# A decode step's page loads, old x, output weights and last stores put in another order

## The chip, the cores and the metric

The kernel runs on one core of a Trainium2 chip, in one launch. The metric is device time in microseconds; the number given for a kernel is the median of its runs. A separate execution is recorded by the hardware profiler, and the rows further down come from it.

## What is computed

Two layers of a decoder trunk, for 512 prompt tokens and for 8 sequences of 8 new tokens each. Every sequence of new tokens attends to 16 cached pages of 128 rows, which a page table places in a pool. Cut to what matters here:

```python
def layer_forward(x, pos, p, ret_s0, ret_chunk, attend):
    h = rmsnorm(x, p['norm_w'])
    z = h @ p['w_in']                       # 1024 -> 3264 columns
    ...                                     # retention on half the heads
    o_a = attend(qn, qp, c, kpe, p)         # latent attention
    y = jnp.concatenate([o_r, o_a], axis=-1) @ p['w_out']
    return x + y, c, kpe, s_new

def mla_attend_sample(...):                 # one of 8 sequences
    c_all  = concat([cache_ckv[layer, pt].reshape(-1, 256), c_s])
    kp_all = concat([cache_kpe[layer, pt].reshape(-1, 64), kpe_s])
    kn = rmsnorm(c_all @ w_kb); v = c_all @ w_vb
    s = qn @ kn.T + qp @ kp_all.T           # then mask, softmax
    return softmax(s * SCALE) @ v
```

## The kernel before

Everything is fp32, and the large products are made of three TensorE products of a high and a low part. Each layer goes through four stages: the input projection in eight column groups; the prompt's attention and the retention; the eight decode sequences over their cached pages; and the output projection in three column groups (344, 340 and 340 columns) over five row tiles. Tiles 0 to 3 are the prompt's, 128 rows each; tile 4, `S_TILE`, holds the 64 new tokens.

**The program of each engine is written out by hand**, and the engines meet at semaphores. All DMAs are issued by SyncE (SP), in program order; a wait holds back everything written behind it.

**The decode stage.** Page buffers are double: `ckv[b]` and `kp[b]` hold the 16 pages of one sequence, sequence s in buffer s mod 2. `load_seq(seq, b, wait)` asks for them in four quarters of four pages. A quarter is four reads of the page table, then, unless `wait` is None, one wait on `pv_ps` (the quarter of the sequence two before has been multiplied by its probabilities, so its pages are free), then eight DMAs: four of 32 KB (`kp`) and four of 128 KB (`ckv`).

TensorE works through a sequence in eight page pairs `q`. In pair `q` it transposes the pages of pair q+1 (`turn_pair`, line 978) and multiplies the keys of pair q (`pair_keys`, line 1003). The softmax of the sequence before is worked off meanwhile: in pair 4 `tail_attend` (line 1031) multiplies its probabilities by its pages and frees its buffer; in pair 6 `tail_turn` (line 1051) transposes the result; in pair 7 the first pages of the next sequence are transposed, and this waits for their DMAs.

**SP's order in the decode stage** is: pages of sequence 0; `wout0` (first column group of the output weights); pages of sequence 1; old x (`z[:, :, 0:D]`, 2 MB of prompt and 256 KB of new tokens, needed for the residual sum at the end of the layer); `wout1` (second column group, four DMAs of 340 KB); in the first layer a wait and the clearing of the layer's semaphores, followed by `fresh`; then a loop over the pages of sequences 2 to 7.

**The output projection.** `out_product(g, t)` makes column group g of tile t. A prompt tile takes 24 matmuls, `S_TILE` 16. VectorE adds a tile to old x (`x_add`, line 2128). For `S_TILE` its high and low rows are summed first: ScalarE copies the low half out of PSUM (`move_out`, line 1560) and VectorE adds twice (lines 2126 and 2128). `store(g)` waits for `S_TILE` of group g and writes the group's columns with two DMAs, one for four prompt tiles and one for `S_TILE`.

Of the kernel before, what the change touches and what calls it, by code (L numbers as in the profile page):

```python
# [30 lines left out]
DEPTH, D, SEQ = 2, 1024, 512  # L31
NB, NT = 8, 8
# [3 lines left out]
TILES = SEQ // P + 1  # L36
S_TILE = TILES - 1
# [14 lines left out]
OG = (0, 344, 684, 1024)  # L52
# [12 lines left out]
def rows(t):  # L65
    return ST if t == S_TILE else P
# [50 lines left out]
def build(nc, x_prompt, x_sample, cache_ckv, cache_kpe, state_ret, page_table, norm_w, w_in, q_a_norm_w,  # L117
# [177 lines left out]
    def sem(name, per_layer=True):  # L295
        s = nc.alloc_semaphore(name)
        if per_layer:
            layer_sems.append(s)
        return s
# [10 lines left out]
        + [(2, t) for t in range(TILES)]  # L310
    NTH = {gt: i + 1 for i, gt in enumerate(OUT_ORDER)}
    N_OUT = len(OUT_ORDER)
    N_W = 4 * (NG + 3)
    N_RAW = NG + 1
    N_Y = 2 * TILES
# [4 lines left out]
    def mix_tile(k):  # L320
# [10 lines left out]
    out_done, state_out, x_out = sem("out_done"), sem("state_out"), sem("x_out", False)  # L331
# [39 lines left out]
    y_ready, y_turned, y_hi, y_lo, out_ps, x_new = (sem(n) for n in  # L371
        ("y_ready", "y_turned", "y_hi_kept", "y_lo_kept", "out_in_psum", "x_new_ready"))
# [8 lines left out]
    X_OUTS = 6  # L381
# [5 lines left out]
    def zc(t, c0, n):  # L387
        return z[0:rows(t), t, c0:c0 + n]
# [3 lines left out]
    def _(sp):  # L392
        yp_t = y_prompt[0].rearrange("(t p) d -> p t d", p=P)
        ys_t = y_sample.rearrange("b t d -> (b t) d")
# [7 lines left out]
        def load_norm(l):  # L402
            spread(norm_b[:, :], norm_w, l, D, norm_in)
# [36 lines left out]
        for L in range(DEPTH):  # L440
            for g in range(1, NG):
                for k in range(4):

                    sp.wait_ge(w_lo_ok, N_W * L + g * 4 + (k - 3))
                    sp.dma_start(raw[:, k, :, :], w_in_t[L][:, 2 * k:2 * k + 2, g * GW:(g + 1) * GW])\
# [31 lines left out]
            def load_seq(seq, b, wait, quarters=range(QUARTERS)):  # L477
                for k in quarters:
                    numbers = [load_page(seq, b, k * QPAGES + n) for n in range(QPAGES)]
                    if wait is not None:  # L480

                        sp.wait_ge(pv_ps, (wait + L * NB) * QUARTERS + (k + 1))
                    for n, v in enumerate(numbers):
                        sp.dma_start(kp[b][:, k * QPAGES + n, :], kpe_rows[bass.ds(v, 1), :, :]  # L484
                                     .rearrange("l p k -> (l p) k")).then_inc(page_in[QUARTERS * b + k], 16)
                        sp.dma_start(ckv[b][:, k * QPAGES + n, :], ckv_rows[bass.ds(v, 1), :, :]  # L486
                                     .rearrange("l p k -> (l p) k")).then_inc(page_in[QUARTERS * b + k], 16)
# [15 lines left out]
            load_seq(1, 1, None)  # L503


            if L:
                sp.wait_ge(x_out, 16 * X_OUTS)
            old_p = yp_t if L else x_prompt[0].rearrange("(t p) d -> p t d", p=P)
            old_s = ys_t if L else x_sample.rearrange("b t d -> (b t) d")
            sp.dma_start(z[:, 0:S_TILE, 0:D], old_p).then_inc(xold_in, 16)  # L510
            sp.dma_start(z[0:ST, S_TILE, 0:D], old_s).then_inc(xold_in, 16)

            for k in range(4):
                sp.dma_start(wout1[:, k, :, :], w_out_t[L][:, 2 * k:2 * k + 2, OG[1]:OG[2]]).then_inc(wout1_in, 16)
            if L + 1 < DEPTH:
# [3 lines left out]
                    if s not in running_sems:  # L519
                        sp.sem_clear(s)  # L520
                sp.sem_inc(fresh, 1)
            with sp.Fori(1, NB // 2) as i:
                load_seq(i * 2, 0, i * 2 - 2)
                load_seq(i * 2 + 1, 1, i * 2 - 1)

# [6 lines left out]
            def store(g):  # L532
                cols = slice(OG[g], OG[g + 1])
                sp.wait_ge(x_new, N_OUT * L + NTH[g, S_TILE])
                sp.dma_start(yp_t[:, :, cols], z[:, 0:S_TILE, cols]).then_inc(x_out, 16)
                sp.dma_start(ys_t[:, cols], z[0:ST, S_TILE, cols]).then_inc(x_out, 16)

            if L + 1 < DEPTH:

                sp.wait_ge(out_ps, N_OUT * L + NTH[0, S_TILE])  # L540
                load_norm(L + 1)
                load_small(L + 1)
                store(0)
                for k in range(4):

                    sp.wait_ge(w_lo_ok, N_W * L + 4 * (NG + 2) + k + 1)
                    sp.dma_start(raw[:, k, :, :], w_in_t[L + 1][:, 2 * k:2 * k + 2, 0:GW]).then_inc(raw_in[k], 16)
            else:
                store(0)
            store(1)  # L550
            store(2)
        sp.wait_ge(x_out, 16 * X_OUTS * DEPTH)


    @block.tensor
    def _(pe):
# [7 lines left out]
        def tile_products(out, t, w_h, w_l, chunks=range(DC), w0=None):  # L564

            for c in chunks:
                if w0 is not None and c % 2 == 0:
                    pe.wait_ge(w_lo_ok, w0 + c // 2 + 1)
                if t == S_TILE:
                    pe.matmul(out, hT_s[:, c, :], w_h(c), start=c == 0, stop=False)  # L570
                    m = pe.matmul(out, hT_s[:, c, :], w_l(c), start=False, stop=c == DC - 1)  # L571
                else:
                    rows_t = slice(t * P, (t + 1) * P)
                    m = product(out, (hT_hi[:, c, rows_t], hT_lo[:, c, rows_t]), (w_h(c), w_l(c)), c == 0, c == DC - 1)
            return m
# [3 lines left out]
        for L in range(DEPTH):  # L579
# [15 lines left out]
            def tile_product(g, t):  # L595
# [7 lines left out]
                for chunks in halves:  # L603
                    if chunks[0]:
                        x_turn(1)
                    m = tile_products(ps[:, BANK[t], 0:GW], t, lambda c: w_hi[w][:, c, :], lambda c: w_lo[w][:, c, :],
                                      chunks, w0=N_W * L if g == 0 and t == 0 else None)
                m.then_inc(z_in_psum, 1)
# [7 lines left out]
            for g in range(1, NG):  # L616
                pe.wait_ge(w_lo_ok, N_W * L + g * 4 + 4)
                for t in range(TILES):
# [478 lines left out]
            def out_chunks(g, t, chunks):  # L1097
                n_cols = OG[g + 1] - OG[g]
                if g == 0:
                    w_h, w_l = w0_hi, w0_lo  # L1100
                else:
                    w_h, w_l = w_hi[W_PAR[g]], w_lo[W_PAR[g]]
                return tile_products(ps[:, BANK[t], 0:n_cols], t, lambda c: w_h[:, c, 0:n_cols],
                                     lambda c: w_l[:, c, 0:n_cols], chunks)

            def out_begin(g, t):
                if g == 0:
                    if t == 0:
                        pe.wait_ge(w_lo_ok, N_W * L + 4 * (NG + 1))
                    pe.wait_ge(y_lo, N_Y * L + 2 * (t + 1))  # L1110

                    if t < 2:
                        pe.wait_ge(kk_kept, 2 * N_PAIR * (L + 1) - 1)
                    elif t < S_TILE:
                        pe.wait_ge(kk_kept, 2 * N_PAIR * (L + 1))
                    else:
                        pe.wait_ge(rp_kept, N_PAIR * (L + 1))
                else:
                    if t == 0:
                        pe.wait_ge(w_lo_ok, N_W * L + 4 * (NG + g + 1))  # L1120
                    pe.wait_ge(x_new, N_OUT * L + NTH[g - 1, t])
                out_chunks(g, t, range(DC // 2))

            def out_end(g, t):
                out_chunks(g, t, range(DC // 2, DC)).then_inc(out_ps, 1)

            def out_product(g, t):
                out_begin(g, t)
                out_end(g, t)
# [36 lines left out]
            out_product(0, S_TILE)  # L1166
            for t in range(1, TILES):
                out_product(1, t)
            for t in range(S_TILE):
                out_product(2, t)  # L1170
            if L + 1 < DEPTH:
                pe.wait_ge(fresh, L + 1)
                x_turn(0)
            out_product(2, S_TILE)


    @block.scalar
    def _(act):
# [11 lines left out]
        for L in range(DEPTH):  # L1190

            def square_x(t):
                if L == 0:
                    act.wait_ge(x_in[t], 16)
                else:
                    act.wait_ge(x_new, N_OUT * (L - 1) + NTH[2, t])
                act.activation(zc(t, D, D), zc(t, 0, D), ACT.Square, accum_out=stat[0:rows(t), t:t + 1])
# [7 lines left out]
            def split(g, chunks=range(4)):  # L1205
                for k in chunks:
# [3 lines left out]
                    if k == 0 and g < 2 and L:  # L1210

                        act.wait_ge(out_ps, N_OUT * (L - 1) + NTH[1 + g, S_TILE])
                    act.wait_ge(raw_in[k], 16 * (N_RAW * L + g + 1))
# [339 lines left out]
                    act.activation(dst[:, 2 * k:2 * k + 2, 0:n], src, ACT.Copy).then_inc(w_hi_ok, 1)  # L1553

            def move_out(g, L):
                act.wait_ge(out_ps, N_OUT * L + NTH[g, S_TILE])
                if g:
                    act.wait_ge(x_new, N_OUT * L + NTH[g - 1, S_TILE])
                n_cols = OG[g + 1] - OG[g]
                act.activation(out_s[:, 0:n_cols], ps[ST:P, BANK[S_TILE], 0:n_cols], ACT.Copy).then_inc(out_s_moved, 1)  # L1560
# [43 lines left out]
    def _(dve):  # L1604
# [18 lines left out]
        for L in range(DEPTH):  # L1623
# [495 lines left out]
            def x_add(g, t, L):  # L2119
                n = rows(t)  # L2120
                n_cols = OG[g + 1] - OG[g]
                dve.wait_ge(out_ps, N_OUT * L + NTH[g, t])
                x = zc(t, OG[g], n_cols)
                if t == S_TILE:
                    dve.wait_ge(out_s_moved, 3 * L + g + 1)
                    dve.tensor_tensor(x, out_s[:, 0:n_cols], x, ALU.add)
                    dve.drain()
                dve.tensor_tensor(x, ps[0:n, BANK[t], 0:n_cols], x, ALU.add).then_inc(x_new, 1)
# [69 lines left out]
            x_add(1, S_TILE, L)  # L2198
            x_add(2, 0, L)
            if L + 1 == DEPTH:  # L2200
                for t in range(1, TILES):
                    x_add(2, t, L)


# [215 lines left out]
```

## Time and profile before

| what | us |
|---|---|
| median of 3 runs (1241.48 to 1242.68) | 1241.63 |
| profiled execution, its own time | 1244.96 |
| its span, first to last instruction | 1243.2 |
| TensorE (PE) busy in it | 1215.2 |
| VectorE, ScalarE, GpSimd busy | 724.2, 527.2, 436.3 |

The profiled execution has 1.76 us around its span, and its own time is 3.33 us above the median of the runs. PE is busy for 98% of the span, with a mean granted clock of 0.996 of full speed, so the kernel goes as fast as PE is fed; what can be won lies in the 28 us in which PE does not work and in the stretches in which its clock is lower.

### The profile page before, as it was taken

The page shows a single profiled execution, that of the slowest core. Times are in us where ns is not written, and L with a number is a line of the kernel's source. Part 1 is how long each engine was busy: PE and PEld are TensorE (multiplying, and loading weights), DVE is VectorE, ACT ScalarE, POOL GpSimd, SP SyncE. Part 2 cuts the span into 40 slices and gives each one's busy share as a digit, 9 for nine tenths or more (in the row PEclk, how much of TensorE's full clock was granted, in tenths as well). Part 3 has the DMA queues.
Part 4 walks back from the last instruction along what each step waited for, and adds up shares of the span by engine and source line. Part 5 has one row for each costly group of instructions (what it writes and reads, how often), then busy time and mean ns, then how long its engine had stood idle before and what let it go on. Part 6 is the DMA issues. An engine that isn't in the chain of part 4 may idle for free.

```text
span 1243.2 us, 26204 instructions
## 1 busy us (share of the span) xinstructions
PE 1215.2 (98%) x8720; PEld 1127.1 (91%) x8720; DVE 724.2 (58%) x1322; ACT 527.2 (42%) x1377; POOL 436.3 (35%) x632
## 2 busy tenths in 40 slices
PE   6999999999989999999999999999999999999998
PEld 6999995768989999999999999867789999999998
DVE  5455746565646666666463465656556566665652
ACT  4311325444645555563242122453455555555520
POOL 1023046432535454541010320554235445454400
PEclk9999999999989999999999999999999999999999
DMA  9331104103462223220733130220045433322021
GB/s 318 115 108 55 54 2 123 37 1 95 131 186 77 78 79 85 75 54 1 260 119 123 55 109 1 76 85 1 13 134 157 130 85 84 84 75 75 21 72 51
DMA packets 127894, 108.32 MB, mean 87 GB/s; under 512 B 45681, under 2 KB 123634, under 8 KB 127794
## 3 DMA queue, kind: packets, MB, share of 16 engines
q1 hardware_dynamic: 127794, 107.08, 28.9%
q8 instruction: 51, 0.84, 0.3%
q14 instruction: 49, 0.40, 0.1%
HBM read 96.12 MB, written 10.91 MB: 86 GB/s over the span
## 4 chain that ended last, share of the span: by engine, by line
PE 81%; SPq 9%; issue 3%; DVE 2%; DMA 2%; ACT 1%; DVEq 1%; POOL 0%; POOLq 0%; ACTq 0%
PE ps L1003 23%; PE ps L560 10%; PE ps L561 10%; PE ps L562 10%; PE ps L978 4%; PE ps L654 3%; SPq L486 3%; SPq L470 3%; PE ps L570 3%; PE ps L571 3%; SPq L484 2%; PE ps L1031 2%; PE ps L1012 1%; PE ps L813 1%; PE ps L667 1%
## 5 line engine op out<-in xcount | busy, mean ns | idle before, releaser
L2049 DVE TENSOR_REDUCE kss<-ksq 128x8 f32<-128x1024 f32 x128 | 156.0, 1219 | 171.1 <-ACT ksq L1525 171.0
L560 PE MATMUL ps<-w_hi,hT_hi 128*128 128x408 f32 (+2 forms) x704 | 242.9, 345 | 1.5 <-DVE hT_lo L1614 1.5
L1525 ACT ACTIVATE ksq<-ps 128x544 f32<-128x544 f32 x256 | 160.1, 625 | 196.3 <-PE ps L1003 195.9
L561 PE MATMUL ps<-w_lo,hT_hi 128*128 128x408 f32 (+2 forms) x704 | 240.0, 341 | 0.0
L562 PE MATMUL ps<-w_hi,hT_lo 128*128 128x408 f32 (+2 forms) x704 | 239.3, 340 | 0.0
L1003 PE MATMUL ps<-wq_hi,cT_hi 128*128 128x272 f32 x1024 | 224.7, 301 | 0.0
L2384 POOL TENSOR_TENSOR krs<-kss_t,cst 128x8 f32<-128x8 f32 x128 | 210.0, 1640 | 20.1 <-issue 4.2
L1003 PE MATMUL ps<-wq_lo,cT_hi 128*128 128x272 f32 x1024 | 212.6, 289 | 0.0
L1003 PE MATMUL ps<-wq_hi,cT_lo 128*128 128x272 f32 x1024 | 212.6, 289 | 0.0
L1003 PEld LDWEIGHTS ps<-wq_lo,cT_hi 128*128 128x128 f32 x1024 | 161.7, 190 | 0.0
L1003 PEld LDWEIGHTS ps<-wq_hi,cT_lo 128*128 128x128 f32 x1024 | 161.4, 189 | 0.0
L1003 PEld LDWEIGHTS ps<-wq_hi,cT_hi 128*128 128x128 f32 x1024 | 160.0, 190 | 0.0
L560 PEld LDWEIGHTS ps<-w_hi,hT_hi 128*128 128x128 f32 x704 | 132.6, 188 | 2.8 <-DVE hT_lo L1614 1.9
L561 PEld LDWEIGHTS ps<-w_lo,hT_hi 128*128 128x128 f32 x704 | 132.9, 189 | 0.1
L562 PEld LDWEIGHTS ps<-w_hi,hT_lo 128*128 128x128 f32 x704 | 132.7, 189 | 0.2
L2377 POOL TENSOR_TENSOR kss_t<-kss,cst 128x8 f32<-128x8 f32 x128 | 27.2, 212 | 246.6 <-DVE kss L2049 246.6
L1220 ACT ACTIVATE z<-ps 64x408 f32<-64x408 f32 x16 | 8.1, 508 | 226.0 <-PE ps L571 226.0
L1512 ACT ACTIVATE cT_hi<-ps 128x512 fp32r<-128x512 f32 x126 | 76.6, 608 | 39.5 <-PE ps L978 39.4
L2041 DVE TENSOR_TENSOR cT_lo<-ps,cT_hi 128x512 fp32r<-128x512 f32 x126 | 86.0, 683 | 5.8 <-ACT cT_hi L1512 5.3
L2209 POOL TENSOR_SCALAR pool_tmp<-stat 128x1 f32<-128x1 f32 (+2 forms) x70 | 17.1, 244 | 194.3 <-ACTq L1198 77.6
L978 PE MATMUL ps<-cst,ckv 128*128 128x128 f32 x504 | 79.0, 280 | 6.2 <-DMA ckv<-in_cache_ckv 4.9
L1652 DVE TENSOR_SCALAR z<-ps 128x408 f32<-128x408 f32 x64 | 35.9, 579 | 81.6 <-PE ps L562 80.2
(209 smaller groups left out, 1989.9 us busy)
## 6 DMA issues: line engine op xcount, KB each, us to landing
ckv<-in_cache_ckv SPq DMA_DIRECT2D x256, 128.0 KB, 2.0
raw<-in_w_in SPq DMA_DIRECT2D x64, 408.0 KB, 4.4
kp<-in_cache_kpe SPq DMA_DIRECT2D x256, 32.0 KB, 1.8
S<-in_state_ret SPq DMA_DIRECT2D x8, 512.0 KB, 6.2
out<-S SPq DMA_DIRECT2D x8, 512.0 KB, 3.2
wout<-in_w_out SPq DMA_DIRECT2D x8, 344.0 KB, 4.5
z<-in_w_out SPq DMA_DIRECT2D x8, 340.0 KB, 10.1
raw<-in_w_out SPq DMA_DIRECT2D x8, 340.0 KB, 4.3
```

The costliest lines, as they stand in the source:

```text
L470: v = sp.value_load(pages[0:1, seq * NPAGE + n:seq * NPAGE + n + 1] if isinstance(seq, int) else pages[0:1, bass.ds(seq * NPAGE + n, 1)], ...
L486: sp.dma_start(ckv[b][:, k * QPAGES + n, :], ckv_rows[bass.ds(v, 1), :, :] .rearrange("l p k -> (l p) k")).then_inc(page_in[QUARTERS * b + ...
L560: pe.matmul(out, a_hi, b_hi, start=first, stop=False)
L561: pe.matmul(out, a_hi, b_lo, start=False, stop=False)
L562: return pe.matmul(out, a_lo, b_hi, start=False, stop=last)
L978: m = pe.transpose(ps[:, 0, (2 * j + c) * P:(2 * j + c + 1) * P], ckv[b][:, 2 * q + j, c * P:(c + 1) * P], ident)
L1003: m = pe.matmul(ps[:, 1 + 2 * j + side, 0:CUT], x, w[:, c, w0:w0 + CUT], start=c == 0 and k == 0, stop=c == KC - 1 and k == 2)
L1512: act.activation(cT_hi[:, par, :, :].rearrange("p a n -> p (a n)"), ps[:, 0, :], ACT.Copy)\
L1525: act.activation(ksq[:, q % 2, j, :].rearrange("p (s c) -> p s c", s=2), ps[:, 1 + 2 * j:3 + 2 * j, 0:CUT], ACT.Square).then_inc(kk_sq, 1)
L2041: dve.tensor_tensor(cT_lo[:, par, :, :].rearrange("p a n -> p (a n)"), ps[:, 0, :], cT_hi[:, par, :, :].rearrange("p a n -> p (a n)").bitc ...
L2049: dve.tensor_reduce(kss[:, hs, 2 * k:2 * k + 2, :], ksq[:, q % 2, :, c0:c0 + HW].rearrange("p j (h k) -> p j h k", h=H), AX.X, ALU.add).th ...
L2384: pool.tensor_tensor(krs[:, hs, c, :], tmp, spread_col(neg_half[:, 0:1]), ALU.pow)\
```

## The change

There are two parts. In SP's program, the pages of sequence 2 are asked for ahead of old x, and those of sequence 3 ahead of `wout1`; the loop starts at the pair of sequences 4 and 5. In the last layer's last column group, the order of the tiles is 0, 1, 2, `S_TILE`, 3 in place of 0, 1, 2, 3, `S_TILE`, on TensorE, on VectorE and in the counts that ScalarE waits for; and each tile is stored by a DMA of its own as soon as it is added.

```diff
+    LAST_TILES = (0, 1, 2, S_TILE, 3)
+
+    def nth(g, t, L):
+        if g == 2 and L + 1 == DEPTH:
+            return N_OUT - TILES + 1 + LAST_TILES.index(t)
+        return NTH[g, t]
...
             load_seq(1, 1, None)
+            load_seq(2, 0, 0)
             if L:
                 sp.wait_ge(x_out, 16 * X_OUTS)
...
             sp.dma_start(z[:, 0:S_TILE, 0:D], old_p).then_inc(xold_in, 16)
             sp.dma_start(z[0:ST, S_TILE, 0:D], old_s).then_inc(xold_in, 16)
+            load_seq(3, 1, 1)
...
-            with sp.Fori(1, NB // 2) as i:
+            with sp.Fori(2, NB // 2) as i:
                 load_seq(i * 2, 0, i * 2 - 2)
                 load_seq(i * 2 + 1, 1, i * 2 - 1)
...
-            store(2)
-        sp.wait_ge(x_out, 16 * X_OUTS * DEPTH)
+            if L + 1 < DEPTH:
+                store(2)
+        for t in LAST_TILES:
+            sp.wait_ge(x_new, N_OUT * (DEPTH - 1) + nth(2, t, DEPTH - 1))
+            dst = ys_t[:, OG[2]:OG[3]] if t == S_TILE else yp_t[:, t, OG[2]:OG[3]]
+            sp.dma_start(dst, zc(t, OG[2], OG[3] - OG[2])).then_inc(x_out, 16)
+        sp.wait_ge(x_out, 16 * (X_OUTS * DEPTH - 2 + TILES))
...
-            for t in range(S_TILE):
-                out_product(2, t)
             if L + 1 < DEPTH:
+                for t in range(S_TILE):
+                    out_product(2, t)
                 pe.wait_ge(fresh, L + 1)
                 x_turn(0)
-            out_product(2, S_TILE)
+                out_product(2, S_TILE)
+            else:
+                for t in LAST_TILES:
+                    out_product(2, t)
...
-                act.wait_ge(out_ps, N_OUT * L + NTH[g, S_TILE])
+                act.wait_ge(out_ps, N_OUT * L + nth(g, S_TILE, L))
...
-                dve.wait_ge(out_ps, N_OUT * L + NTH[g, t])
+                dve.wait_ge(out_ps, N_OUT * L + nth(g, t, L))
...
-                for t in range(1, TILES):
+                for t in LAST_TILES[1:]:
                     x_add(2, t, L)
```

SP's program of the first layer, where the last page DMA of sequence 1 (`kp1`, `ckv1`) stands, before the change. The `ISA` rows of line 520 are the wait and the clearing of semaphores.

```order
L486 DMA ckv1_118<-in_cache_ckv 128x256
L510 DMA z_49<-in_x_prompt 128x4x1024
L511 DMA z_49<-in_x_sample 64x1024
L514 DMA z_49<-in_w_out 128x2x340 x4
L520 ISA [waits half_scores_ready]
L520 ISA x74
L522 UNCONDITIONAL_BRANCH
L522 ISA
L470 TENSOR_LOAD pages_64
```

The same place after the change, with the first page-table read and the first wait and DMAs of sequence 2; old x stands behind its 32 DMAs:

```order
L493 DMA ckv1_118<-in_cache_ckv 128x256
L477 TENSOR_LOAD pages_64
...
L491 ISA [waits latents_attended_a_quarter]
L491 DMA kp0_119<-in_cache_kpe 128x64
...
L493 DMA ckv0_117<-in_cache_ckv 128x256
L518 DMA z_49<-in_x_prompt 128x4x1024
L519 DMA z_49<-in_x_sample 64x1024
L477 TENSOR_LOAD pages_64
```

And where the loop is entered after the change, behind the last page of sequence 3; the page buffer asked for next (`kp0`) is that of sequence 4:

```order
L493 DMA ckv1_118<-in_cache_ckv 128x256
L523 DMA z_49<-in_w_out 128x2x340 x4
L529 ISA [waits half_scores_ready]
L529 ISA x74
L531 UNCONDITIONAL_BRANCH
L531 ISA
L477 TENSOR_LOAD pages_64
...
L491 ISA [waits latents_attended_a_quarter]
L491 DMA kp0_119<-in_cache_kpe 128x64
```

Old x moved behind the 32 DMAs of sequence 2, and the output weights with the 75 semaphore instructions moved from the entry of sequence 2's pages to that of sequence 4's. Each layer's program has 64 page DMAs more outside the loop; the number that is executed is the same.

The end of VectorE's program before, from the first column group 2 tile of 64 rows onward:

```order
L2128 TENSOR_TENSOR z_49<-ps,z_49 128x340 [waits out_in_psum] x4
L2126 TENSOR_TENSOR z_49<-z_49 64x340 [waits out_sample_lo_moved,out_in_psum]
L2128 TENSOR_TENSOR z_49<-ps,z_49 64x340
L2395 UNCONDITIONAL_BRANCH
```

and after the change:

```order
L2145 TENSOR_TENSOR z_49<-ps,z_49 128x340 [waits out_in_psum] x3
L2143 TENSOR_TENSOR z_49<-z_49 64x340 [waits out_sample_lo_moved,out_in_psum]
L2145 TENSOR_TENSOR z_49<-ps,z_49 64x340
L2145 TENSOR_TENSOR z_49<-ps,z_49 128x340 [waits out_in_psum]
L2412 UNCONDITIONAL_BRANCH
```

The two adds of `S_TILE` (64 rows) moved ahead of the last add of a prompt tile. The last stores on SP became, after the change:

```order
L565 DMA out_0<-z_49 128x340 [waits x_new_ready] x3
L565 DMA out_1<-z_49 64x340 [waits x_new_ready]
L565 DMA out_0<-z_49 128x340 [waits x_new_ready]
L2412 UNCONDITIONAL_BRANCH [waits x_out]
```

Four stores of 170 KB and one of 85 KB stand there in place of one of 680 KB and one of 85 KB.

## Rows read from the trace of the kernel before

**Rows 1.** The page: busy time of each engine.

```profile
PE 1215.2 (98%) x8720; PEld 1127.1 (91%) x8720; DVE 724.2 (58%) x1322; ACT 527.2 (42%) x1377; POOL 436.3 (35%) x632
```

**Rows 2.** Waits, whole run: engine, line, awaited, total us, times, longest.

```profile
PE ps L978 <- DMA ckv<-in_cache_ckv: 4.9, 2, 3.3
```

**Rows 3.** PE timeline, first layer: start, us, instruction [idle before <-releaser].

```profile
359.87 1.11 PE L978 MATMUL ps<-cst,ckv 128*128 128x128 f32 x4 [3.27 <-DMA ckv<-in_cache_ckv]
```

**Rows 4.** Windows around that stall: us, busy by engine, PEclk, DMA share, GB/s.

```profile
356.60:359.87 3.27, 0.01 (x1) 0.01 (x1) 1.22 (x1) 0.27 (x3) 1.59 (x3) 0.87 0.47 130
359.87:366.36 6.49, 6.49 (x32) 6.49 (x32) 0.89 (x3) 1.48 (x4) 0.44 (x1) 0.54 0.40 102
366.36:370.09 3.73, 3.73 (x34) 3.73 (x33) 1.82 (x2) 2.20 (x7) 1.46 (x3) 1.00 0.25 69
```

**Rows 5.** Windows from one line-1031 group to the next; layer one, then two.

```profile
346.27:385.52 39.25, 35.98 (x302) 35.02 (x305) 20.88 (x33) 18.64 (x58) 16.60 (x25) 0.91 0.47 136
385.52:418.50 32.98, 32.98 (x301) 32.13 (x305) 20.78 (x33) 18.57 (x58) 16.53 (x25) 1.00 0.30 81
...
959.85:994.74 34.89, 33.30 (x302) 32.35 (x305) 20.88 (x33) 18.65 (x58) 16.60 (x25) 1.00 0.52 153
```

**Rows 6.** SP timeline, first layer, behind the last page of sequence 1.

```profile
340.12 1.93 SPq L510 DMA_DIRECT2D z<-in_x_prompt  x1
...
342.67 2.29 SPq L514 DMA_DIRECT2D z<-in_w_out  x4
352.52 0.35 SPq L484 DMA_DIRECT2D kp<-in_cache_kpe  x1
```

**Rows 7.** The chain that ended last, just behind: start, us, what.

```profile
357.31 2.43 DMA ckv<-in_cache_ckv
```

**Rows 8.** SP timeline in the loop: first and last DMAs of sequences 3, 4.

```profile
386.30 0.34 SPq L484 DMA_DIRECT2D kp<-in_cache_kpe  x1
...
389.91 0.33 SPq L486 DMA_DIRECT2D ckv<-in_cache_ckv  x1
...
410.65 0.33 SPq L486 DMA_DIRECT2D ckv<-in_cache_ckv  x1
...
419.30 0.35 SPq L484 DMA_DIRECT2D kp<-in_cache_kpe  x1
```

**Rows 9.** PE timeline, where sequence 3's first pages are used.

```profile
395.59 0.64 PE L978 MATMUL ps<-cst,ckv 128*128 128x128 f32 x4
```

**Rows 10.** Tile ckv: all its DMAs, issue time on SP, then landing.

```profile
L486 SPq DMA_DIRECT2D ckv<-in_cache_ckv x256: 332/333/2052, 285.0 to 1152.7; - x128
DMA to landing us min/median/max: 1.9/2.0/6.9
```

**Rows 11.** The chain and PE timeline, second layer, third sequence's first pages.

```profile
965.55 6.10 DMA ckv<-in_cache_ckv
971.76 0.65 PE L978 MATMUL ps<-cst,ckv 128*128 128x128 f32 x4 [1.59 <-DMA ckv<-in_cache_ckv]
```

**Rows 12.** Window of the large loads, second layer; columns as in rows 4.

```profile
955.00:970.00 15.00, 15.00 (x150) 14.15 (x148) 8.68 (x15) 7.99 (x25) 7.73 (x10) 1.00 1.00 309
```

**Rows 13.** Timeline of the end: PE, ACT, DVE, SP.

```profile
1236.98 0.31 PE L571 MATMUL ps<-w_lo,hT_s 128*128 128x340 f32 x1
1237.33 0.45 ACT L1560 ACTIVATE z<-ps 64x340 f32<-64x340 f32 x1 [17.07 <-PE ps L571]
...
1238.46 0.50 DVE L2128 TENSOR_TENSOR z<-ps,z 64x340 f32<-64x340 f32 x1
1238.99 0.39 SPq L535 DMA_DIRECT2D out<-z  x1
1239.43 0.51 SPq L536 DMA_DIRECT2D out<-z  x1
```

**Rows 14.** SP's own waits at the end, same columns as rows 2.

```profile
SPq L2395 <- DMA out<-z: 2.8, 1, 2.8
```

**Rows 15.** The chain: a 256 KB store with the queue to itself.

```profile
923.04 2.60 DMA out<-S
```

## The prediction

> **What bounds the kernel now.** I read the page first: PE works for 1215.2 of 1243.2 us [rows 1], so only what makes PE wait, or lowers its clock, or follows its last matmul, can move the time. The table of waits then says which of PE's waits the change can touch: line 978, the transposes of fresh pages, waited for page DMAs twice, 4.9 us in all, 3.3 the longest [rows 2]. The timeline places them: once in each layer, both times at the first pages of the third sequence (sequence 2). PE stood still for 3.27 us before 359.87 in the first layer [rows 3] and for 1.59 us before 971.76 in the second [rows 11].
>
> Windows over that place show a second loss. In the first layer the granted clock was 0.87 of full during the stall, 0.54 in the 6.49 us after it, and 1.00 again from 366.36 [rows 4]: PE had fallen from 2.4 to about 1.2 GHz. A page pair that takes 3.73 us at the full clock took 6.49 there, 2.76 us more. In the second layer, after 1.59 us of standstill, the clock stayed at 1.00: the window that holds the second layer's stall reads 1.00 throughout [rows 5].
>
> The cleanest measure is the period of the decode stage, from one group of line 1031 to the next. It is 32.98 us where nothing disturbs it, and the next one, whose end is 451.54, is 33.04, so I take 33.01. Around the third sequence it is 39.25 us in the first layer and 34.89 in the second [rows 5]. **The excess is 6.24 us and 1.88 us, 8.12 together**; in the first, 3.27 is standstill, 2.76 slow clock and 0.2 the restart.
>
> Why were the pages late? In the first layer SP issued old x from 340.12, `wout1` from 342.67, then worked through the semaphore clearing and the page table until its first page DMA at 352.52 [rows 6]. The last `ckv` DMA of the quarter went out at 357.31 and landed 2.43 us later [rows 7]. The buffer had been free since about 347: `tail_attend` began at 346.27 [rows 5], and in the loop the first DMA follows it by 0.78 us (386.30 after 385.52) [rows 5, 8]. So SP's order held the pages back, not the buffer. In the second layer, without the clearing, the last `ckv` DMA was issued at 965.55, but took 6.10 us to land [rows 11], against a median of 2.0 [rows 10]: it stood behind 3.6 MB of old x and `wout1`, while the DMA engines were busy for the whole stretch (share 1.00, 309 GB/s) [rows 12].
>
> **The pages of sequence 2.** They will be asked for right behind those of sequence 1, that is at 340.12 in place of old x; SP reads four page numbers and then waits until the first quarter is free, at 346.27 + 0.78 = 347.05. From then on a quarter takes what it takes in the loop: first DMA to last `ckv` DMA 3.61 us (386.30 to 389.91) [rows 8], landing 2.0 [rows 10]. Landed: 352.7. PE needs them when its standstill began, 359.87 - 3.27 = 356.60 [rows 3], so 3.9 us are to spare. The loop's own margin agrees: needed at 395.59 [rows 9], landed at 389.91 + 2.0 = 391.9, 3.7 us to spare. The second layer's stall began at 970.17 [rows 11] and its pages would land at 959.85 + 0.78 + 3.61 + 2.0 = 966.2: 4.0 to spare. Both stalls go, and with the first the slow clock. I take the full excess, 8.12 us; not less, because nothing but the pages separates those two periods from the others, and not more, because PE works for all of 32.98 us in an undisturbed period [rows 5].
>
> **Old x and `wout1`, later.** Old x now goes out behind the last DMA of sequence 2. A sequence's 32 DMAs take 24.35 us (386.30 to 410.65) [rows 8], so at about 347.05 + 24.35 = 371.4; with its 2.5 us of issue [rows 6] and four page numbers SP is ready for sequence 3 at about 377. That sequence's release is at 386.30 - 6.24 = 380.06. No delay. The data are first used by the sum at the end of the layer, behind all eight sequences. Its 2.25 MB at the 309 GB/s of [rows 12] take 7.3 us and are through by about 381, as the first pages go out. Cost: nothing; the cover is those 3 us and the margin of 3.7.
>
> **The semaphore clearing, later.** This is the step with least room. From the first `wout1` DMA to the first page DMA behind the clearing SP took 352.52 - 342.67 = 9.85 us [rows 6]. After the change that stands between the last DMA of sequence 3, at 410.65 - 6.24 = 404.4 plus 0.4, and the first of sequence 4: 414.65. The buffer is free for it at 419.30 - 6.24 = 413.06 [rows 8]. So those pages start 1.6 us late. The first quarter at a loop entry also took longer, 4.79 us to its last `ckv` issue (352.52 to 357.31) against 3.61: 1.2 more. Late by 2.8 in all, of the 3.7 there are: it is hidden, with 0.9 us left. Later quarters are needed one every two page pairs, twice 3.73 us [rows 4], and go out faster than that. ScalarE, GpSimd and PE wait for `fresh` only at the end of the layer. Second layer: no clearing, no delay.
>
> **The end.** PE's last matmul begins at 1236.98 and ends at 1237.29, whichever tile it belongs to, since the same 112 matmuls are issued. Before, ScalarE's copy at 1237.33 and VectorE's two adds followed, the second from 1238.46 to 1238.96; the stores were issued at 1238.99 and 1239.43 [rows 13], SP waited 2.8 us for them [rows 14], from 1239.94 to 1242.74, and the span ended at 1243.2, 5.91 us after PE. After, tile 3 needs one add: 1237.33 to 1237.84, store issued at 1237.87. `S_TILE` is through by then: its copy and adds take 1.7 us and tile 3's 24 matmuls 3.8.
>
> No row shows a store of 170 KB with the queue to itself. The nearest is one of 256 KB, 2.60 us [rows 15]; from below I take the 2.0 of a 128 KB page [rows 10], from above the 85 KB store at the end, 1242.74 - 1239.43 = 3.31, though it went behind 680 KB. With 2.60 the data are down at 1240.47 and the span ends 0.46 later, at 1240.93: **a gain of 2.27 us**, between 1.56 and 2.87. The three earlier stores in pieces are 3.8 us apart or 2.5 (one tile's matmuls) and end before it.
>
> The Trainium skill speaks against splitting a store: "DMA: Bandwidth & Descriptors", the rules for kernel authors, wants small transfers coalesced, and its anatomy of one DMA gives a fixed part of about 2.0 us to each. By its formula a 174 KB store takes 2.4 us, an estimate from that page, and the end would gain 2.5; the four fixed parts would be paid at the same time as PE's matmuls. The trace's 680 KB store does not show the two parts apart.
>
> **The sum.** 6.24 + 1.88 + 2.27 = 10.39 us off the profiled execution: span 1232.8, own time 1234.6. The runs of before have a median 3.33 us below that execution; taking the same difference off, **1241.63 - 10.4 = 1231.2**. Its own range, from the end's bounds and a few tenths at each stall, is 1230.2 to 1232.4.
>
> **Rivals.**
> *The slow clock is not in the timed runs (0.20).* The profiled execution was 3.33 us slower than the runs, and 2.76 of that may be this very stretch. For it: the size, and that the second layer's standstill of 1.59 us did not lower the clock [rows 5, 11], so a standstill need not. Against: recording an execution costs something by itself, and this stall is twice as long as the harmless one. Then the gain is 7.6 and the time 1234.0. "TensorE: Matmul & The Clock Gate", what's actually happening, in the Trainium skill, says that the moment at which the clock is judged runs freely, so the same kernel can differ from run to run. One execution with one fall and one without agrees and proves nothing.
>
> *A new stall at sequence 4 in the first layer (0.12).* The 0.9 us left are an estimate, and one `ckv` issue sometimes took up to 2.05 us in place of 0.33 [rows 10]. One more such hiccup (1.7) makes PE wait 0.8: 1232.0; with the clock falling too, 2.76 more, 1234.8.
>
> *The order was not what held the pages (0.04).* Then both stalls stay and only the end gains: 1239.4, within 0.2% of before.
>
> *Slower (0.03).* The large loads now go out in the middle of the stream of pages. If pages land behind them as in the second layer before, 6.10 us, they outlast the 2.0 + 3.7 us that there are. There are four such places (old x and `wout1`, two layers). The point that decides is a landing of more than 5.7 us together with a fallen clock: each stall as heavy as the first layer's costs 6.24, and two give back 12.5, 1243.7. Against it: the pages are asked for 6 us or more after the load's issue, not 3.
>
> **How the numbers follow.** The forecast has 0.58, and 0.03 is left for what I haven't seen. The range takes in the clock rival and most of the stall: 1229.8 to 1235.6. A measurement of this kernel tells about 0.2%, 2.5 us, from no change; forecast, clock and stall all lie beyond it: faster 0.91, same 0.06, slower 0.03.
>
> **What the changed kernel's profile would show.** Line 978 waits for no `ckv` DMA, or under 1 us; PEclk is 1.00 in every window from 300 to 1230; periods of 33.0 us at both third sequences; the first page DMAs of sequence 2 about 0.8 us behind line 1031's group; those of sequence 4 in the first layer about 1.6 us late; from PE's last matmul to the end 3.6 us. A wait at line 978 near 416 would show the clearing was not hidden; a timed gain near 7.6 with the profile as forecast would point to the clock; a last store of over 3.3 us would make the end's term wrong.

## The result, and the profile after

The changed kernel took 1234.45 us (median of 4 runs, 1234.08 to 1234.51), the kernel before 1241.56 (4 runs, 1240.82 to 1242.68): a ratio of 0.9941, interval 0.9924 to 0.9959, or 7.1 us less. The profiled execution of the changed kernel has a span of 1232.7 us and a time of 1234.51, that is 10.5 us less than the profiled one of before. The prediction had 10.4 for the profiled pair and gave the same 10.4 to the runs.

The page of the changed kernel, busy times and granted clock (line numbers are 7 to 17 higher than before from here on):

```profile
span 1232.7 us, 26123 instructions
PE 1212.6 (98%) x8720; PEld 1124.7 (91%) x8720; DVE 724.0 (59%) x1322; ACT 526.9 (43%) x1377; POOL 437.4 (35%) x632
PEclk9999999999999999999999999999999999999999
```

In the row of the granted clock a 9 stands for 90% or more, and no slice falls below it. PE is busy 2.6 us less than in [rows 1] with the same 8720 matmuls: that is about the 2.76 us of the slow stretch, which is gone. The whole list of PE's waits has no line for a page DMA any more. Windows of one period each, from one group of line 1045 (1031 before) to the next, columns as in [rows 4]:

```profile
346.73:379.77 33.04, 33.04 (x299) 32.19 (x298) 20.79 (x33) 18.57 (x58) 16.57 (x25) 1.00 0.51 153
379.77:412.75 32.98, 32.98 (x299) 32.13 (x298) 20.78 (x33) 18.58 (x58) 16.57 (x25) 1.00 0.44 123
954.07:987.11 33.04, 33.04 (x299) 32.19 (x298) 20.81 (x33) 18.57 (x58) 16.59 (x25) 1.00 0.50 151
```

The first and the third answer to the 39.25 and 34.89 us of [rows 5]: 6.21 and 1.85 us less, with the clock at 1.00. SP's timeline in the first layer:

```profile
347.57 0.33 SPq L491 DMA_DIRECT2D kp<-in_cache_kpe  x1
...
351.18 0.33 SPq L493 DMA_DIRECT2D ckv<-in_cache_ckv  x1
...
370.96 0.43 SPq L518 DMA_DIRECT2D z<-in_x_prompt  x1
...
380.62 0.34 SPq L491 DMA_DIRECT2D kp<-in_cache_kpe  x1
...
403.69 0.33 SPq L493 DMA_DIRECT2D ckv<-in_cache_ckv  x1
404.06 1.97 SPq L523 DMA_DIRECT2D z<-in_w_out  x4
413.61 0.36 SPq L491 DMA_DIRECT2D kp<-in_cache_kpe  x1
```

Sequence 2's first page DMA is 0.84 us behind the group at 346.73, where it was 6.25 us behind its own in [rows 5, 6]. Old x and the output weights stand where the forecast had them. Sequence 4's first page DMA, which was to be 1.6 us late, is 0.08 us late (412.75 + 0.78 = 413.53). The timeline of the end of the kernel:

```profile
1229.42 0.32 PE L576 MATMUL ps<-w_hi,hT_lo 128*128 128x340 f32 x1
1229.77 0.51 DVE L2145 TENSOR_TENSOR z<-ps,z 128x340 f32<-128x340 f32 x1 [2.12 <-PE ps L576]
1230.31 0.34 SPq L565 DMA_DIRECT2D out<-z  x1
```

SP's last wait, as in [rows 14]:

```profile
SPq L2412 <- DMA out<-z: 1.6, 1, 1.6
```

And the last store among the DMA issues: count, size, time from issue to landing:

```profile
out<-z SPq DMA_DIRECT2D x1, 170.0 KB, 1.9
```

From PE's last matmul (1229.74) to the end of the span it is 2.96 us, against 5.91 in [rows 13]: 2.95 less, where 2.27 was forecast. The 170 KB store landed in 1.9 us, just under the lowest of the three values that the forecast weighed (2.0), not in the 2.60 of [rows 15].

So the two profiles differ where and by what the prediction said: 6.21 + 1.85 + 2.95 = 11.0, less 0.46 us by which the changed kernel came later to its decode stage (346.73 against 346.27). What did not come true is that the timed runs differ as much.

### The profile page after: what moved, and what is told of

The parts are those of the page before. It is cut to its first block, busy times and chain, and to the rows that moved or that the text cites. A ratio compares the mean times of both kernels' runs of the same rounds, so it can differ in the third digit from the quotient of the medians.

```text
span 1232.7 us, 26123 instructions
## 1 busy us (share of the span) xinstructions
PE 1212.6 (98%) x8720; PEld 1124.7 (91%) x8720; DVE 724.0 (59%) x1322; ACT 526.9 (43%) x1377; POOL 437.4 (35%) x632
## 4 chain that ended last, share of the span: by engine, by line
PE 93%; DVE 3%; ACT 2%; issue 1%; DMA 1%; DVEq 1%; POOL 0%; SPq 0%; POOLq 0%; ACTq 0%
PE ps L1017 30%; PE ps L574 10%; PE ps L575 10%; PE ps L576 10%; PE ps L992 5%; PE ps L668 3%; PE ps L584 3%; PE ps L585 3%; PE ps L1045 2%; PE ps L1026 2%; PE ps L827 1%; PE ps L850 1%; PE ps L828 1%; PE ps L681 1%; PE ps L996 1%; PE ps L659 1%
```

## The experiments

Theory A: the runs of before differ among themselves, in how long PE waits for sequence 2's pages and whether its clock falls; the profile of before was one of the heavier ones. Theory B: the stalls are in every run alike, and recording the first profile cost 3.3 us by itself. Each row of the table is one kernel with its runs. The kernels came in three sets; those of one set ran beside each other and share the runs of before. All three sets carry the same chip number, the first comparison above carries none.

| set | kernel | median (lowest to highest), runs | before, runs | ratio (interval) |
|---|---|---|---|---|
| 1 | before again | 1241.11 (1237.01 to 1245.75), 12 | 1240.26 (1236.79 to 1248.11), 35 | 1.0005 (0.9987 to 1.0023) |
| 1 | pages only | 1237.41 (1237.05 to 1237.82), 12 | same | 0.9969 (0.9956 to 0.9982) |
| 1 | end only | 1239.45 (1235.52 to 1242.06), 12 | same | 0.9982 (0.9963 to 1.0001) |
| 1 | pages, layer 0 | 1238.09 (1237.14 to 1240.24), 12 | same | 0.9980 (0.9965 to 0.9996) |
| 2 | changed again | 1233.82 (1233.67 to 1234.25), 5 | 1239.71 (1237.90 to 1244.02), 21 | 0.9955 (0.9940 to 0.9969) |
| 2 | clearing later | 1237.51 (1236.62 to 1238.80), 11 | same | 0.9980 (0.9970 to 0.9990) |
| 2 | clearing three times | 1242.15 (1241.13 to 1242.67), 11 | same | 1.0020 (1.0011 to 1.0029) |
| 2 | one store | 1235.53 (1235.22 to 1237.15), 6 | same | 0.9971 (0.9958 to 0.9983) |
| 3 | split, old order | 1235.58 (1234.88 to 1236.21), 6 | 1239.18 (1236.97 to 1243.43), 23 | 0.9961 (0.9948 to 0.9975) |
| 3 | pages only, again | 1237.45 (1236.41 to 1237.83), 12 | same | 0.9979 (0.9970 to 0.9989) |
| 3 | pages, layer 1 | 1240.68 (1236.98 to 1243.21), 12 | same | 1.0000 (0.9987 to 1.0014) |
| 3 | sequence 3 in place | 1234.14 (1233.75 to 1234.92), 6 | same | 0.9951 (0.9938 to 0.9964) |

**The kernel before, again.** No edit.

> The kernel before, unchanged, run and profiled once more. Theory A, the slow clock behind the first layer's stall comes in some executions only: its runs have a mean granted clock of 1.00 in most and about 0.996 in a few, the ones at 0.996 some 2.8 us longer (1241.5 against 1244.3). Theory B, the slow clock is in every execution and only the recording of the first profile cost 3.3 us: every run shows a clock near 0.996 and a time of 1241 to 1243. Either way the ratio to the kernel before is 1.000.

It scattered over 8.7 us. Its profile, a span of 1239.3 us, is of the same program as the first. The stalled instruction in PE's timeline:

```profile
358.96 0.93 PE L978 MATMUL ps<-cst,ckv 128*128 128x128 f32 x4 [1.90 <-DMA ckv<-in_cache_ckv]
```

The whole run's only wait of that kind in the table of waits:

```profile
PE ps L978 <- DMA ckv<-in_cache_ckv: 1.9, 1, 1.9
```

And the windows behind the stall, columns as in [rows 4]:

```profile
358.96:364.29 5.33, 5.33 (x32) 5.33 (x32) 0.89 (x3) 1.48 (x4) 1.67 (x2) 0.68 0.35 95
364.29:368.01 3.72, 3.72 (x33) 3.72 (x33) 1.82 (x2) 2.20 (x7) 1.45 (x3) 1.00 0.17 48
```

The first layer's stall is 1.90 us in place of 3.27, the slow stretch costs 5.33 - 3.72 = 1.6 us in place of 2.76, and the second layer has no stall. The three differ from [rows 3, 4, 11] by 1.37 + 1.15 + 1.59 = 4.1 us; the spans differ by 3.9. Each run lists its mean granted clock, and the 79 runs of before of the three sets fall like this:

| granted clock | runs | median us (lowest to highest) |
|---|---|---|
| 0.995, 0.996 | 6 | 1244.23 (1242.93 to 1248.11) |
| 0.997 | 19 | 1241.70 (1239.78 to 1243.39) |
| 0.998 | 18 | 1240.27 (1237.87 to 1242.88) |
| 0.999 | 31 | 1238.70 (1236.79 to 1240.22) |
| 1.000 | 5 | 1238.04 (1237.90 to 1239.54) |

The first profile of before, at 0.996 and 1244.96, is one of the heaviest. That fits theory A as it is put here. The version that was expected ahead of these runs, a clock of 1.00 in most and 0.996 in a few, does not fit: the runs do not fall into two groups, and 25 of the 79 are at 0.997 or lower. Theory B falls with the scatter, and by two more numbers: this kernel's own profiled execution took 1241.07 us, 0.04 from the median of its 12 runs, and that of the changed kernel (1234.51) lies 0.06 us from its median. So recording does not cost 3.3 us by itself.

**The pages alone.** The part of the diff that moves the page loads in SP's program; the end as before.

> Only the first part of the change: pages of sequences 2 and 3 asked for earlier, the end of the kernel as before. Theory A (no slow clock in the timed runs of before): 1241.5 - 3.48 - 1.88 = 1236.2 or a little above. Theory B (slow clock in all of them): 1241.5 - 8.1 = 1233.4. Profile in both: no wait for page DMAs on TensorE, span 1235.0.

1237.41, 2.85 us below before in the median: far from theory B's 8.1, and less than the 5.3 that theory A had here, which took both standstills of the first profile for those of every run. What tells more is the scatter: 0.8 us in 12 runs, where before has 11 in 35. Its profile has no wait for a page and its span, 1235.5, is 3.8 us below that of before again. The fastest runs of before, 1236.79 to 1237.5, are no slower than this kernel: they fit an execution in which the pages came in time without any help.

**The end alone.**

> Only the second part: last layer's tile order and a store per tile, the page loads as before. By the profiles the end gains 2.3 to 2.4 us: 1239.2 in both theories. If part of the whole change's missing 3.3 us lies in the end (the recorder lengthens the old stores more than the new), it gains under 1 us: above 1240.5. Stalls of 3.3 and 1.6 us stay.

The expected 2.3 us are neither seen nor excluded: 0.8, with an interval from 4.6 us gained to 0.1 lost, because the stalls scatter. Its profile has a first-layer stall of 2.21 us and again none in the second layer. This run settles nothing on the end; the later sets do.

**The pages in the first layer only, and in the second only.**

```diff
+            if L == 0:                     # second kernel: if L:
+                load_seq(2, 0, 0)
...
+            if L == 0:                     # second kernel: if L:
+                load_seq(3, 1, 1)
...
-            with sp.Fori(1, NB // 2) as i:
+            with sp.Fori(2 if L == 0 else 1, NB // 2) as i:
```

> The page loads moved in the first layer only, everything else as before. Theory A: gain 3.3 to 3.5 us, 1238.1. Theory B: 6.24 us, 1235.3. The second layer's wait of 1.6 us for page DMAs stays in the profile; granted clock 1.00 from start to end.

> The page loads moved in the second layer only, the rest as before. The second layer's wait was 1.6 us in the first profile and none in two others, so the median gains 0 to 1.3 us against before, and the scatter of before (5 us and more, granted clocks from 0.996 to 1.00) stays, since the first layer's stall makes it. Rival: if the second layer made the scatter, the runs lie within 1 us.

The first layer alone gave 2.2 of the 2.85 us. The second alone gave nothing that shows (a ratio of 1.0000, with an interval of 1.6 us to either side), and kept the scatter (6.2 us, clocks 0.996 to 0.999). The profile of the first has 0.53 us of wait in the second layer, where 1.6 was expected; the profile of the second has 1.72 us in the first. So most of the median gain of the page loads is the first layer's, and most of the scatter comes from there. Not all of it: with the old order in the second layer alone 12 runs still spread over 3.1 us, against 0.8 with both layers changed.

**The changed kernel, again.**

> The whole change once more, with more runs. Theory A' (before's stalls differ from run to run, the change takes them away): the 12 runs lie within 1 us of each other, around 1234.5, while the runs of before on the same chip spread over 5 us or more; 2.9 us below the pages-only kernel's 1237.4. Rival (the chip was quiet in the one run of each that was profiled, and both kernels scatter alike): the changed kernel's runs spread over several us too.

Five runs within 0.6 us, all at a clock of 1.00, beside 21 of before over 6.1 us. The gain in this set is 5.9 us, not 7.1: from the first comparison to this one the changed kernel moved by 0.6, before's median by 1.9. With 4 runs of a kernel that scatters over several us, the 7.1 is itself partly chance.

**The clearing behind the pages.** The kernel before, with only this moved:

```diff
+            load_seq(2, 0, 0)
+            load_seq(3, 1, 1)
             if L + 1 < DEPTH:
                 sp.wait_ge(ds_ok, 2 * NB * L + 1)
                 ...                        # the 75 semaphore instructions
-            with sp.Fori(1, NB // 2) as i:
+            with sp.Fori(2, NB // 2) as i:
```

> The kernel before with the pages of sequences 2 and 3 moved ahead of the 75 semaphore instructions only: old x and second output weights stay in front of them. If the semaphore instructions were what held the first layer's pages (theory S), TensorE's wait there falls from 1.9 to 3.3 us to about 0 to 1.3 (first page DMA near 348, landing up to 6.1 us behind the large loads), its clock stays at 1.00, and the median falls by 2 to 3 us against before. If the large loads were (theory L), the pages land as late as before and the median stays within 0.5 us. The second layer, without clearing, stays as it was: a wait of 0 to 1.6 us.

2.2 us below before, as expected if the semaphore instructions held the pages (theory S there), though old x and the output weights stay in front. The chain of the kernel before shows where SP was meanwhile: the clearing is line 520, the page table line 470.

```profile
345.01 0.03 SPq L520
...
349.17 0.03 SPq L522
...
349.35 0.28 SPq L470
...
352.52 0.35 SPq L484
```

The clearing took 4.2 us, from 345.01 to 349.17, more than the stall of 3.27. SP's timeline with the clearing moved: the first page DMA, and the last `ckv` DMA of the first quarter,

```profile
342.16 2.12 SPq L514 DMA_DIRECT2D z<-in_w_out  x4
347.33 0.35 SPq L484 DMA_DIRECT2D kp<-in_cache_kpe  x1
...
350.98 0.33 SPq L486 DMA_DIRECT2D ckv<-in_cache_ckv  x1
```

The first page DMA is 5.2 us earlier than in [rows 6], 4.2 of them the clearing and 0.7 an earlier end of the output weights' issue, and PE waits for no page. So in the first layer it was the clearing that made PE wait. The 3.6 MB in front of the pages were not harmless, though: the last `ckv` DMA of the quarter took 4.8 us to land in place of 2.0, at about 355.8, and PE came for the pages at 356.63. That leaves 0.8 us to spare, where the changed kernel had 3.7 (landed at 351.18 + 2.0, wanted at 356.88).

**The clearing three times over.** The changed kernel, with `for s in 3 * layer_sems`.

> The changed kernel with the semaphores cleared three times over in the first layer (150 instructions, about 8.6 us more, nothing else). In the changed kernel's profile the first page DMA of sequence 4 went out 0.1 us after it could, and its pages had about 3.7 us to spare. Then TensorE waits near 423 for 8.7 - 3.7 = 5.0 us, its granted clock falls to about half for 6 us behind it as after the 3.3 us stall, some 2.8 us more: 1234.5 + 7.8 = 1242.3. If the clock falls only under the recorder or rarely, 1239.5. If the pages have more room than I count, under 1237.

1242.15 where 1242.3 was expected, 11 runs within 1.5 us, ten of them at a clock of 0.997. The windows of stall, slow stretch and next pair:

```profile
422.15:427.63 5.48, 0.00 (x1) 0.01 (x1) 1.22 (x1) 0.28 (x3) 2.03 (x3) 0.90 0.47 120
427.63:433.97 6.34, 6.34 (x31) 6.34 (x32) 0.89 (x3) 1.48 (x4) 0.00 (x0) 0.55 0.38 103
433.97:437.70 3.73, 3.73 (x33) 3.73 (x33) 1.82 (x2) 2.20 (x7) 1.45 (x3) 1.00 0.14 42
```

The first page DMA of sequence 4 went out at 421.65, 9.04 us after it could (411.83 + 0.78), and PE waited 5.48: the pages had 3.6 us to spare, against the prediction's 3.7. Stall and slow clock are 5.48 + 2.61 = 8.1 us, the timed runs lie 8.3 above the changed kernel. So a slow stretch such as [rows 4] shows is in timed runs too; one of 11 had a clock of 0.999, and it was 0.6 us below the median, not 2.6, which I can't explain.

**One store, and the old order.** The changed kernel with the four prompt tiles' last columns in one store; and with `LAST_TILES = (0, 1, 2, 3, S_TILE)`.

> The changed kernel with the last column group of tiles 0 to 3 in one store of 680 KB behind tile 3, as before, and the sample tile's store ahead of it; the tile order stays changed. If the order gives what lies between the last matmul and the last store's issue (1.1 us) and the splitting the shorter landing, this kernel lies 1.5 to 1.9 us above the changed one: 1236.2. If splitting does nothing, 1234.5.

> The changed kernel with the tile order of before (sample tile last) and a store per tile. With order and splitting as separate terms: the copy and second add of the sample tile are back (1.1 us), its 85 KB store has the queue to itself, so 1.1 to 1.2 us above the changed kernel: 1235.0. If the splitting only pays together with the order, 1236.7 as for the old end.

One store: 1.7 us above the changed kernel. Last stores of its profile:

```profile
out<-z SPq DMA_DIRECT2D x1, 680.0 KB, 3.5
```

against 1.9 for the piece: 1.6 us. Old order: 1.4 us above its neighbour of set 3, sequence 3 in place, where 1.1 to 1.2 over the changed kernel was expected. In its profile the last issue comes 1.70 us after PE's last matmul, against 0.57 in the changed kernel, and its last store,

```profile
out<-z SPq DMA_DIRECT2D x1, 85.0 KB, 2.4
```

took 0.5 us longer to land than the 170 KB piece. The end has two terms that add, 1.7 for splitting and 1.4 for the order, 3.1 together.

**Pages only, again, beside sequence 3 in place.** The second is the changed kernel with `load_seq(3, 1, 1)` moved behind the clearing.

> The first part alone once more, to have it on one chip with the kernels of this call. If the end is worth in the timed runs what it is in the profiles (2.95 us), it lies 2.9 us above the kernel with sequence 3 in place and 1.7 above the one with the old order: 1236.8. If the end is worth less without the recorder, under 2 us above. Its runs lie within 1 us of each other.

> The changed kernel with the pages of sequence 3 behind the second output weights and the semaphore clearing, as in the order of before; only sequence 2's are ahead of old x. SP should be ready for sequence 3's first quarter at about 381, 0.4 us behind its release, with 3.7 us to spare: no wait, same time as the changed kernel, 1233.8 to 1234.4. If moving sequence 3 was needed, TensorE waits at its first pages, near 389, and it lies 1 us or more above.

The two differ by 3.3 us, the whole worth of the end in timed runs (2.95 in the profiles), if sequence 3's place is worth nothing. That it is worth little shows so: 1234.14 in set 3 and 1233.82 for the changed kernel in set 2 differ by less than the changed kernel did from the first comparison to set 2, and the profile has no wait for a page. The two kernels did not run beside each other. No version was faster than the changed kernel.

## Why the prediction was right and where it was off

**The place and the cause of the stalls: right.** SP's order held the pages; with them first, both waits and the slow stretch are gone, to 0.1 us of the forecast in the profiles. That it was the clearing in the first layer is shown by the kernel that moved only that. In the second layer, which has no clearing, the large loads in front of the pages are the cause by the trace of before alone (6.10 us to land, [rows 11]); no run took them apart.

**The sum for the profiled execution: right**, 10.39 against 10.5, with one term too small (the end, 2.27 for 2.95, since the row of the 256 KB store was the wrong neighbour for a 170 KB one; that store also had a 128 KB page load 0.38 us in front of it, so it did not have the queue to itself) and the later arrival at the decode stage against it.

**The step that failed** is "taking the same difference off" the median of the runs. It held that the profiled execution's stalls were in every run. In the runs they were worth less: the pages gave 2.85 and 1.7 us in the median of sets 1 and 3, not 8.12, and in the first comparison 7.1 less the end's 3.1 to 3.3 leaves about 4. The forecast's own rival, the slow clock not in the timed runs, gave 1234.0 and came nearest, and it is this rival that the stated range reaches up to; the forecast itself, 1231.2, was 3.2 us too low. That the rival came so near is in part luck. Its gain of 7.6 us holds against the four runs of before in the first comparison, not against the 5.9 of set 2; the end, booked 0.7 to 1 us too small, hid part of it. Its ground against itself, that recording costs something, is not borne out: the two profiled executions compared above lie within 0.1 us of their kernels' medians. And its picture was too simple. It isn't one stall with or without a fall: the stall itself was 3.27, 1.90, 2.21 and 1.72 us in four profiles with the old page order in the first layer, its slow stretch cost 2.76 in the first and 1.6 in the other three, and the second layer's stall was 1.59 in the first profile, 0.53 in that of the pages in the first layer only, and absent in those of before again and of the end alone. The 2.21 us stand in the profile of the end alone, the 1.72 in that of the pages in the second layer only:

```profile
358.70 0.85 PE L990 MATMUL ps<-cst,ckv 128*128 128x128 f32 x4 [2.21 <-DMA ckv<-in_cache_ckv]
359.14 0.65 PE L982 MATMUL ps<-cst,ckv 128*128 128x128 f32 x4 [1.72 <-DMA ckv<-in_cache_ckv]
```

**What makes the stall differ** the traces show in part. In all four, one page DMA of sequence 2's first quarter took 1.03 to 1.47 us to issue in place of 0.33; I call such an issue a hiccup. In SP's timeline of the kernel before, first profile:

```profile
354.12 1.47 SPq L486 DMA_DIRECT2D ckv<-in_cache_ckv  x1
```

and of the kernel before again:

```profile
354.59 1.03 SPq L484 DMA_DIRECT2D kp<-in_cache_kpe  x1
```

The landing behind them was 2.43 and 2.00 us. These two terms make 0.9 of the 1.37 us by which the two stalls differ; PE's own arrival, 0.46 us later in the second, makes the rest. The hiccup at this place is no accident of one execution: 12 of the 14 traces have a DMA issue of 1.03 us or more that begins between 353.5 and 355.7, whatever SP issues there, and 11 have one between 324.9 and 326.4. Only its length and the DMA that it strikes change. What makes it is open. In the old order it falls into the one quarter that is already late; with the pages ahead it falls into a later quarter, which has time to spare, and PE does not wait. Executions above 1245 us were seen in timed runs only; no trace shows what they waited for, so that stays open.

**The clearing at sequence 4: right that it was hidden**, with more room than I gave it: 0.08 us late in place of 1.6, and without the 1.2 of a slow first quarter. The 1.2 was the hiccup of 1.47 us at 354.12, which I had taken for the cost of the place. Of the 1.6, 1.3 came from sequence 3's 32 DMAs: they take 24.35 us from first to last inside the loop [rows 8], which I carried over, but 23.07 (380.62 to 403.69) now that they are written out ahead of it. The other 0.3 is the stretch from `wout1` to the first page, 9.55 us in place of 9.85.

**The second layer's term, 1.88**, is in the two profiles, but worth 0 (alone) to 0.7 us (on top of the first layer's) in the medians, neither of them clear of the scatter.

**Splitting the last store** gained 1.7 us in the timed runs: the earlier pieces land under matmuls and only the last one is waited for. The Trainium skill, in "DMA: Bandwidth & Descriptors", rules for kernel authors, wants small transfers coalesced; at this place the opposite paid. By the formula in the same page's anatomy of one DMA, which the Trainium skill fits on DMAs that GpSimd issues, the last store takes 2.4 us, an estimate; the trace has 1.9 for this one, issued by SP, and the measurement decides.

## What to carry to other kernels

A wait in one profile is a sample. Before its length is booked, see whether the runs of the kernel agree with the profiled one: here a profiled time 3.3 us above the median said that they did not. Where an issuing engine serves a loop with a deadline, put the loop's next request ahead of bulk loads and housekeeping that nobody waits for, and count the margin (3.7 us here), since it also takes up the hiccups: the scatter went from 11 us in 35 runs to 0.8 and 1.4 us in two times 12 with the pages moved. A request that is ahead of the housekeeping but behind the bulk loads came in time too, with 0.8 us to spare. At the end of a kernel, let the piece with the shortest way out come last, and store it alone.

## What was not expected of the hardware

A single DMA issue on SP took up to 2.05 us in place of 0.33 [rows 10], at other instructions from one execution to the next, but near the same moments of the span (about 325.5 and 354.5 us in most traces). The granted clock behind a stall did not fall alike: 0.54 over 6.49 us after 3.27 us of standstill [rows 4], 0.68 over 5.33 after 1.90, 0.68 over 5.32 after 2.21, 0.68 over 5.30 after 1.72, 0.55 over 6.34 after 5.48, and not at all after 1.59 [rows 5, 11]. They cost 2.76, 1.6 (three times) and 2.6 us: the longest stall was not the one that cost most, and 1.72 us of standstill in the first layer cost 1.6 where 1.59 us in the second cost nothing.

Sequences written out ahead of the loop need less of SP than in it: from the first to the last of 32 page DMAs 23.0 us (sequence 2 of the changed kernel's first layer) against 24.4 in the loop (sequence 4), with no hiccup in either.
